# Value and gate columns of a decoder's input projection by seven products per pair of token tiles, with the dilated values kept in DRAM

## What is computed

```python
h = adaLN(RMSNorm(x), c)
proj = h @ w_in            # NSA q | NSA k/v x3 | 24 gates | dilated q | k | v | merge gates
q_n, kv_n, gate_n, qkv_d, merge = jnp.split(proj, IN_SPLITS, axis=-1)
gate_n = sigmoid(gate_n)                       # 3 branches x 8 heads
kc, vc = compress_blocks(...k...), compress_blocks(...v...)   # MLP over blocks of 32 tokens
o_c, o_s = compressed and selected attention(q_n, kc, vc, kv_n[sel])
o_w = banded_attention(q_n, kv_n[win], window 512)
o_nsa = gate_n[0]*o_c + gate_n[1]*o_s + gate_n[2]*o_w
o_dil = dilated_attention(qkv_d)               # 3 groups: strides 1, 4, 16; 4 heads each
x += gate1 * (merge of both mixers); x += gate2 * MoE(adaLN(RMSNorm(x)))
```

## Time and profile before

| | us |
|---|---|
| three executions | 1752.1, 1758.1, 1759.5 (median 1758.1) |
| the profiled execution | 1753.5 |
| its span in the profile | 1751.6 |
| PE busy | 1628.7 (93%) |
| DVE, ACT, POOL busy | 646.8, 406.9, 176.3 |
| projections, queries and keys | about 49 to 290 |
| projections, value part | about 290 to 424 |
| NSA attention | about 426 to 664 |

### The profile page before, as it was taken

The page is one execution under the profiler, slowest core; times in us unless marked ns, Lnnn a source line. Parts: engine busy times, 40 slices in busy tenths (PEclk is TensorE's granted clock), DMA queues, the critical chain, the costliest instruction groups (busy, mean ns, idle before and its releaser), DMA issues. The chain is left out here.

```text
span 1751.6 us, 37114 instructions
## 1 busy us (share of the span) xinstructions
PE 1628.7 (93%) x16025; PEld 1069.8 (61%) x16025; DVE 646.8 (37%) x1594; ACT 406.9 (23%) x908; POOL 176.3 (10%) x220
## 2 busy tenths in 40 slices
PE   5999999999999998999999999999999999998783
PEld 3444445898777786644444445556777767666562
DVE  3533332001767666766655455561000000000003
ACT  4000000001666666610010003221121122111112
POOL 1205000000111110000000000001111111111100
PEclk9999999999999999999999999989999999999996
DMA  9874224131011107334452172169999999999996
GB/s 341 258 230 112 74 84 146 37 104 42 2 44 44 33 2 237 111 111 129 120 145 83 37 280 85 68 258 390 391 383 384 394 387 382 396 392 397 406 385 229
DMA packets 146623, 356.07 MB, mean 203 GB/s; under 512 B 14751, under 2 KB 94231, under 8 KB 121851
## 3 DMA queue, kind: packets, MB, share of 16 engines
q1 hardware_dynamic: 120656, 305.50, 47.0%
q0 software_dynamic: 12656, 28.01, 6.0%
q10 hardware_dynamic: 13148, 20.18, 3.3%
HBM read 320.53 MB, written 45.36 MB: 209 GB/s over the span
## 5 line engine op out<-in xcount | busy, mean ns | idle before, releaser
L2635 PE MATMUL psum<-sb_m_xT,sb_m_ring 128*64 128x64 f32 (+2 forms) x4096 | 152.0, 235 | 22.0 <-issue 17.7
L2635 PEld LDWEIGHTS psum<-sb_m_xT,sb_m_ring 128*64 128x64 f32 x4096 | 147.8, 140 | 35.6 <-issue 34.7
L2384 ACT ACTIVATE sb_m_xT<-psum,sb_rowmod 128x64 f32<-128x64 f32 (+2 forms) x256 | 81.7, 424 | 216.3 <-PE psum L2623 216.3
L2519 DVE TENSOR_TENSOR sb_m_hT<-psum,sb_m_sg 128x256 f32<-128x256 f32 (+2 forms) x32 | 15.3, 477 | 308.9 <-PE psum L2635 308.9
L748 PE MATMUL psum<-sb_vD,sb_room 128*128 128x512 f32 x240 | 104.7, 593 | 0.2 <-DVE sb_vD L685 0.2
L2635 PE MATMUL psum<-sb_m_xT,sb_front 128*64 128x64 f32 (+2 forms) x2560 | 94.5, 236 | 9.9 <-issue 7.3
L2635 PEld LDWEIGHTS psum<-sb_m_xT,sb_front 128*64 128x64 f32 x2560 | 92.4, 142 | 17.2 <-issue 16.9
L1008 ACT ACTIVATE sb_d_probs<-sb_d_probs,sb_d_nmax 128x640 f32<-128x640 f32 (+7 forms) x128 | 92.9, 735 | 1.6 <-DVE sb_d_nmax L1048 1.0
L2642 PE MATMUL psum<-sb_m_ring,sb_m_hT 128*64 128x512 f32 (+2 forms) x256 | 84.5, 611 | 5.6 <-DMA sb_m_ring<-in_exp_w_dram 4.7
L780 PE MATMUL psum<-sb_b_wvd,sb_rows 128*128 128x256 f32 x384 | 88.9, 394 | 0.0
L780 PEld LDWEIGHTS psum<-sb_b_wvd,sb_rows 128*128 128x128 f32 x384 | 84.9, 286 | 3.3
(11 more groups left out here) (384 smaller groups left out, 2408.8 us busy)
## 6 DMA issues: line engine op xcount, KB each, us to landing
sb_m_ring<-in_exp_w_dram SPq DMA_DIRECT2D x48, 2048.0 KB, 34.4
sb_front<-in_exp_w_dram SPq DMA_DIRECT2D x30, 2048.0 KB, 33.8
sb_rows<-in_exp_w_dram SPq DMA_DIRECT2D x18, 2048.0 KB, 36.5
sb_g_ada<-in_ada_w_dram SPq DMA_DIRECT2D x16, 1024.0 KB, 5.3
d_qk<-sb_n_b_sel ACTq DMA_DIRECT2D x20, 512.0 KB, 3.2
sb_front<-in_w_in_dram SPq DMA_DIRECT2D x16, 512.0 KB, 5.4
sb_front<-d_qk SPq DMA_DIRECT2D x15, 512.0 KB, 7.5
sb_n_b_sel<-in_w_in_dram SPq DMA_DIRECT2D x10, 512.0 KB, 8.9
```

The source lines that it names most:

```text
L2384: last = act.activation(dst[:, kk, 0:w], src, ACT.Identity, scale=k.rowmod[:, 0, kk:kk + 1], bias=k.rowmod[:, 1, kk:kk + 1])
L2635: mm = pe.matmul(k.psum[part, which, c * w:(c + 1) * w], view[:, kk, first:first + 2 * CAPS - 1:2], x[:, kk, 0:w], start=(kk == 0), stop=( ...
```

## The change

The value part now also uses seven products in place of eight. It pairs token tile t with tile t + 4 (the two halves of the tokens), the two halves of the channels, and two sets of columns: sets 0 and 1 for the first four pairs (268 columns: 256 values and 12 gates), sets 2 and 3 for the last four (256 columns). The tokens are in natural order everywhere, and the same token sums serve, so `vD` keeps them to the end of the stage. The sums of weights are made by DVE (`v_sums`), for sets 2 and 3 in the midst of the second pair, one of them at the fifth. ACT copies only M1; DVE adds up everything else, into `vS` for set 0 and into four staging buffers for sets 1 to 3, one buffer per product C11, C12, C21, C22. SP stores these to a DRAM array `d_v`, 24 stores of 128 KB, and DVE waits for a buffer's last store before it writes it again. The dilated order is made when the values are read back: 24 loads with 256 bytes per head and token, issued by SP in the NSA stage behind the bias tables of the second pair of heads.

The compression now stands after the fourth pair (its hidden layer) and the fifth (its outputs), and its weights are fetched by SP. The NSA keys, the queries and the first bias tables are issued by SP after the fifth pair's stores. POOL's filling of the ones column of `vD` moves into the NSA stage, where DVE waits for it, and an exponential on a spare column ends ACT's part of the projections.

```diff
-RV = 2 * P + 3 * NSA_H
+RG = 3 * NSA_H // 2
+RV = 2 * P + RG
...
+            sp.wait_ge(s_done, done(npairs - 1, M4))
+            sp.wait_ge(s_used, used(npairs - 1, C21))
+            for kv in range(2):
+                sp.dma_start(w1c[:, kv], k.cmp_w1[0, kv].rearrange("(l p) n -> p l n", p=P)).then_inc(s_cw, 16)
+                sp.dma_start(w2c[:, kv], k.cmp_w2[0, kv].rearrange("(c p) n -> p c n", p=P)).then_inc(s_cw, 16)
             for s in range(2):
                 sp.wait_ge(s_store[s], 16 * npairs)
...
+            for v in range(NV):
+                for c in (C11, C22, C12, C21):
+                    if set_of(v, c) > 0:
+                        t = v % HT + out_tile[c]
+                        sp.wait_ge(s_vused, vused(v, c))
+                        sp.dma_start(k.d_v[set_of(v, c) - 1, t * P:(t + 1) * P, :], staged(c, v)
+                                     ).then_inc(s_vst[SLOT[c]], 16)
+                if v == HT:
+                    sp.wait_ge(s_hid, 4)
...
+                    for c in (C21, C22):
+                        sp.wait_ge(s_vst[SLOT[c]], 16 * stores_of(c, HT - 1))
+                    sp.wait_ge(s_table, 1)
+                    ahead.load_bias(sp, k, 0)
...
+            for v in range(NV):
+                n = width[v // HT]
+                act.wait_ge(s_v, vdone(v, M1))
+                if v >= 1:
+                    act.wait_ge(s_vused, vused(v - 1, U2))
+                act.copy(vm1[:, 0:n], k.psum[:, vbank(v, M1), 0:n]).then_inc(s_vm1, 1)
...
+            act.activation(ahead.last[:, RV:RV + 1], k.vecT[:, 0:1], ACT.Exp).then_inc(s_gates, 1)
...
+            def v_sums(grp):
+                a11, a12, a21, a22 = (x[grp][:, HK * h:HK * (h + 1)] for x in (vx, vy) for h in range(2))
+                dve.wait_ge(s_wv[grp], (64, 32)[grp])
+                sem = s_vsums[grp]
+                dve.tensor_tensor(s1s[grp], a21, a22, ALU.add).then_inc(sem, 1)
+                dve.wait_ge(sem, 1)
+                dve.tensor_tensor(s2s[grp], s1s[grp], a11, ALU.subtract).then_inc(sem, 1)
+                dve.tensor_tensor(a21, a11, a21, ALU.subtract).then_inc(sem, 1)
+                if grp == 0:
+                    dve.wait_ge(sem, 2)
+                    dve.tensor_tensor(s4s[0], a12, s2s[0], ALU.subtract).then_inc(sem, 1)
...
+                def put(c, i, src):
+                    tile = t + out_tile[c]
+                    if grp == 0:
+                        cols = slice(RG, 2 * RG) if c in (C21, C22) else slice(0, RG)
+                        dve.tensor_tensor(graw[:, tile, cols], ps(i)[:, 256:RV], src[:, 256:RV], ALU.add)
+                    if set_of(v, c) == 0:
+                        dve.tensor_tensor(vS[:, tile, :, 0:DH], heads(ps(i)), heads(src), ALU.add).then_inc(s_vused, 1)
+                        return
+                    if stores_of(c, v) >= 2:
+                        dve.wait_ge(s_vst[SLOT[c]], 16 * (stores_of(c, v) - 1))
+                    dve.tensor_tensor(staged(c, v), ps(i)[:, 0:256], src[:, 0:256], ALU.add).then_inc(s_vused, 1)
...
+                if n >= 4:
+                    was, j = divmod(n - 4, 7)
+                    pe.wait_ge(s_vm1 if j == M1 else s_vused, was + 1 if j == M1 else vused(was, last_use[j]))
+                for kk in range(HK):
+                    mm = pe.matmul(k.psum[:, vbank(v, i), 0:width[grp]], x[:, kk, t * P:(t + 1) * P], w[:, kk, :],
+                                   start=(kk == 0), stop=(kk == HK - 1))
...
+            def load_values(sp):
+                for x, stores in enumerate((NT // 2, NT // 2, NT, NT)):
+                    sp.wait_ge(k.s_vst[x], 16 * stores)
+                v0, v1, v2 = (k.d_v[g].rearrange("s (h d) -> s h d", d=DH) for g in range(DIL_G))
+                for t in range(NT):
+                    r, b = divmod(t, 2)
+                    sp.dma_start(vD[:, 0, t, :, 0:DH], v0[t * P:(t + 1) * P]).then_inc(k.s_vd, 16)
+                    sp.dma_start(vD[:, 1, t, :, 0:DH], v1[512 * b + r:512 * b + r + 509:4]).then_inc(k.s_vd, 16)
+                    sp.dma_start(vD[:, 2, t, :, 0:DH], v2[t:t + 8 * (P - 1) + 1:8]).then_inc(k.s_vd, 16)
...
             for i in range(1, PAIRS):
                 if i >= 2:
                     sp.wait_ge(s_biased, before[2 * NT * (i - 1)])
                 ahead.load_bias(sp, k, i)
+                if i == 1:
+                    load_values(sp)
...
             dve.wait_ge(s_clear, 4)
+            dve.wait_ge(s_ones, 1)
```

More of the change, by code:

```diff
@@ L573, in stage_projections, with staged, set_of, stores_of @@
         last_use = {M6: U2, M5: U5, M7: U3, M2: C11, M3: C12, M4: C21}
-        vjobs = [(s, t) for s in range(4) for t in range(NT)]
-        CMP_AT, OUT_AT = 9, 14
+        HT, HK = NT // 2, KD // 2
+        NV = 2 * HT
+        SPLIT = HT - 1
+        flat = spare[:, 0:4, :].rearrange("p a t -> p (a t)")
+        wvy_flat = wvy[:, :, :].rearrange("p k c -> p (k c)")
+        three = lambda at, n: [at[:, HK * n * i:HK * n * (i + 1)].rearrange("p (k c) -> p k c", k=HK) for i in range(3)]
+        vx, vy = [wva, wvd[:, 0]], [wvy, wvd[:, 1]]
+        width = [RV, 256]
+        s1s, s2s, s4s = zip(three(flat, RV), [stage[0].rearrange("p a (k c) -> p (a k) c", k=2),
+                                              stage[1].rearrange("p a (k c) -> p (a k) c", k=2),
+                                              wvy_flat[:, 0:HK * 256].rearrange("p (k c) -> p k c", k=HK)])
+        vm1, vu2, vu5 = (g2row[:, RV * i:RV * (i + 1)] for i in range(3))
+        vu3 = ahead.last[:, 0:RV]
+        SLOT = {C11: 0, C12: 1, C21: 2, C22: 3}
+        def staged(c, v):
+            if v < HT:
+                return ahead.b_sel[0][1][:, 256 * SLOT[c]:256 * (SLOT[c] + 1)]
+            return room[:, 512 * SLOT[c] + 256:512 * SLOT[c] + 512]
+        out_tile = {C11: 0, C12: HT, C21: 0, C22: HT}
+        def set_of(v, c):
+            return 2 * (v // HT) + (c in (C21, C22))
+        vbank = lambda v, i: 4 + (7 * v + i + 2) % 4
+        vdone = lambda v, i: 7 * v + i + 1
+        vused = lambda v, i: 7 * v + i + 1
+        def stores_of(c, v):
+            return sum(1 for w in range(v + 1) if set_of(w, c) > 0)
         block = k.block(mem)
@@ L644, in _ @@
                               ).then_inc(s_store[1], 16)
[L645 to L656, removed]
+            for v in range(NV):
[4 more added lines that the diff above has]
+                act.copy(vm1[:, 0:n], k.psum[:, vbank(v, M1), 0:n]).then_inc(s_vm1, 1)
+                if v == SPLIT:
                     for kv in range(2):
```

190 lines of the change are left out of this document (121 added, 69 removed).

## The result

The changed kernel took 1746.3 us (median of 7 runs, 1741.3 to 1750.3), the kernel before 1755.2 us on the same chip (7 runs, 1752.1 to 1759.5). The ratio is 0.9943, 95% interval 0.9927 to 0.9959: 8.9 us or 0.57% faster. Forecast were 1745.3 us, 1734 to 1753, and "faster" with 0.70. The profiled execution took 1748.9 us, with a span of 1747.1 against 1751.6.

What follows compares the result with a forecast made beforehand. PE was taken to bound the value part, without idle time there. The terms -19.3 + 0.6 + 5.3 + 2.8 + 0.2 gave -10.4 us, from a mean of 1755.7 to 1745.3 us, range 1734 to 1753.

Steps and rivals of the forecast that it cites:

- Products: PE's matmuls in the value part: 224 with tokens in a row take 99.4 us in place of 118.74, -19.3 us.
- About 5: Value part: the share of the products' 19.3 us gain that comes from strided weight loads, in us.
- First pair: Value part, first pair: PE waits for DVE's weight sum s2, some 1.3 us per sum; +0.6 us, bounds 0 and 1.5.
- DVE and ACT per pair: Value part: DVE's sums, under 4 us beside 12 us of PE per pair, and ACT's one copy cost nothing.
- Wait in the seventh pair: PE waits for M2's bank while DVE awaits a store queued behind SP's fourteen loads; +5.3 us, bounds 0 and 8.
- The ground given for it: SP's queue works in order: line 595's four loads landed after 12.7 to 14.9 us, an empty queue's store after 3.1.
- Clock: Behind the seventh pair's wait the granted clock falls to 1.2 GHz, as at NSA's start; +2.8 us, bounds 0 and 3.3.
- End and start: Value stage's end and NSA's start: SP's last store +0.1 and POOL's fifth fill +0.1, together +0.2 us.
- Reading back: NSA stage: 24 loads of 12,288 pieces cost nothing, taking 12 us by bytes or 24 by pieces.
- My bound of 31 ns: Readback in NSA: time per piece on a DMA engine, from SP's queue at 44 to 101 us, pieces of about 505 bytes.
- The doubling to 50 us: Readback in NSA: by the rule for pieces below 512 bytes, an estimate doubles the pieces' time to some 50 us.
- The rival, bias tables too late for the third pair of heads: NSA, SP's queue: the values' loads block these tables; at 6 us each PE waits 31 us, 1776 us; chance 3%.

Runs made afterwards that it cites:

- The kernel with two sets of buffers: The change with a second set of four staging buffers and semaphores for the sixth and eighth pair; 1735.9 us, 0.9884 of the kernel before.
- the stores on ACT: The change with the stores of the sixth to eighth pair issued from ACT's queue, one set of buffers; 1741.3 us, 0.9919 of the kernel before.
- the two comparisons: The change against the kernel before, timed on two chips: 1746.3 against 1755.2 us (0.9943), and 1741.8 against 1754.9 us (0.9923).
- filling the wait: The change with five idle matmuls of 512 columns ahead of M3 of the seventh pair; 1744.0 us, 0.9939 of the kernel before.
- before again: The kernel before, unchanged, run once more on another chip for a second profile; median 1754.9 us, profiled execution 1753.9 us.
- Two kernels with other values in the mixers: Two sets of buffers with the readback replaced by constant 0.5: 1989.7 us; the kernel before with sets 2 and 3 in natural token order: 2000.4 us.

## Why the prediction was right

The forecast's mechanism came about step by step, and each term of the sum has its measured counterpart. One thing it didn't foresee, in NSA, and there the sum was helped by luck (below).

- **Products, -19.3:** measured 4 x 12.65 + 112 x 0.431 = 98.9 us in place of 118.7, -19.8. The kernel with two sets of buffers, where only the first pair's wait is left, shows the same: its value part is 134.2 - 115.0 = 19.2 us shorter than before. The matmuls came 0.452 and 0.428 to 0.431 us apart, where I had 0.454 and 0.433. "About 5" for the strided loads were 5.4, measured by themselves.
- **First pair, +0.6:** 0.43 us, on line 775 as named; the sums took 1.27 us each (forecast: some 1.3).
- **DVE and ACT per pair at nothing:** in PE's rows of the value part no other wait for DVE or ACT is left.
- **Wait in the seventh pair, +5.3:** 5.27 us, and 5.32 the second time. The parts fit too: the loads held SP for 9.8 us (372.19 to 381.99; forecast 9.6), the store landed 23.6 us after the first load's issue (forecast 24.1), and PE went on at 396.4, forecast 394.8 with a start that lay 2.1 us earlier. The ground given for it was weaker than it reads: four loads that land late show full engines as well as an order in the queue. It took the stores on ACT to tell the two apart.
- **Clock, +2.8:** it fell, as the rows of the NSA start suggested, but cost 1.9 us. This was the term that was most off. The low phase was as long as at the start of NSA before, 6.8 us in both places; but there PE was busy nearly throughout (5.7 us by my reading), while here the first 2.6 us fell into the wait and only 4.2 us of M3 and M4 were slowed.
- **End and start, +0.2:** 416.22 - 415.12 = 1.1 us lie between the idle product's end and NSA's first matmul, 0.88 before: +0.2.
- **Reading back, nothing:** leaving it out changed nothing in NSA. The 24 loads of 12,288 pieces were issued within 18 us and landed after 3.3 us in the median:

```profile
DMA packets 13569, 5.10 MB, mean 94 GB/s; under 512 B 13035, under 2 KB 13049, under 8 KB 13561
...
q1 hardware_dynamic: 13561, 4.99, 37.1%
...
sb_vD<-d_v SPq DMA_DIRECT2D x24, 128.0 KB, 3.3
```

These are the DMA rows of 416 to 470 us: 37.1% of 54 us on 16 engines for 13,561 packets is 23.6 ns a packet. My bound of 31 ns held. The Trainium skill, "DMA: Bandwidth & Descriptors", Specifications, says that pieces below 512 bytes don't reach line rate, since the engine then reads, modifies and writes. On the rate the trace agrees: 256 bytes in 23.6 ns are 10.8 GB/s on an engine, 174 on all 16, while the fourteen loads moved 387 GB/s from 392 to 394 us; of the way in which it comes about no run here tells. The doubling to 50 us was my own step on top of it, and the trace doesn't bear it out. The rival, bias tables too late for the third pair of heads, didn't occur: the last of the 24 loads was issued by 437, the tables of the third pair at 473.1, and those of the fourth, which go out when the third pair starts, at 535.4.

Put together, the measured terms make -19.8 + 0.4 + 5.3 + 1.9 + 0.2 = -12.0 us, the forecast was -10.4, and the two comparisons gave -8.9 and -13.1. NSA took 1.2 us longer than in the first execution before, which the forecast had at nothing, and with it the sum is -10.8. So two misses of over a microsecond, on the terms of the value part and on NSA, nearly cancel; that the total came within 1.0 us of the forecast is in part luck, and executions of one kernel differ by more. (The four executions that the forecast starts from have a mean of 1755.8, not 1755.7; it changes nothing.)

Two further points. The first is NSA. Its matmuls are the same in all these kernels, and its length goes with the time that the clock was at half there (the table above). Windows of the change, in which NSA begins at 416.2, and of the kernel before's second execution, in which it begins at 425.3:

```profile
422.00:426.00 4.00, 4.00 (x32) 0.50 1.06 260
426.00:430.00 4.00, 4.00 (x42) 0.76 0.84 189
```

```profile
425.00:429.00 4.00, 1.83 (x17) 1.00 0.66 226
429.00:433.00 4.00, 3.76 (x46) 1.00 0.67 230
```

In that second execution the clock didn't fall at all in NSA, and the stage took 238.1 us; in the first it was at half for 6.8 us and took 240.4. So one and the same kernel differs by 2.3 us in this place. Both executions of the change have the longest low phase, 10.2 us; filling the wait, which takes away the earlier fall and leaves the rest as it is, gave 6.8. This speaks for the reading that the fall in the value part prolongs the one at NSA's start. With one execution of each kernel, and 0, 3.4 or 6.8 us among those without an earlier fall, it is not proven.

The second is the end, 3 us shorter in the first profile of the kernel before than in all others. It has not been explained; it has nothing to do with the change, as before again shows (573.2).

## What to carry to other kernels

Where a matmul kernel is bound by PE without gaps, count records and their spacing, and look at the weight loads' own length: strided tokens made matmuls of 256 columns 10% slower (0.472 against 0.431 us). A small store that someone waits for should not stand behind large loads in one queue. A second set of buffers was the surest remedy here; another engine's queue worked, with 1.2 us to spare, and brought its own waits with it. The rearrangement through DRAM (3 MB) cost nothing that could be seen, issued behind what is needed next and with a whole stage before its use. And where stages are compared between executions, read the granted clock beside them: here differences of up to 3.5 us in NSA go with it.

## What the runs showed of the hardware

- With a wait of 5.3 us TensorE's granted clock went from 1.00 to 0.50 (2.4 to 1.2 GHz), which cost 1.9 us beyond the wait. With five idle products within it the clock stayed at 1.00, and with a wait of 2.2 us by itself too.
- At the start of NSA, with the same matmuls each time, the clock was at 0.50 for 0 to 10.2 us, and the stage took 238.1 to 241.6 us accordingly; two executions of one kernel had 0 and 6.8.
- A store of 128 KB took 1.7 us where nothing else moved, 7.9 to 10.4 us from ACT's queue beside SP's fourteen loads, and 13.8 us in SP's queue behind the same loads. From ACT's queue a store issued 3 us after a load landed 6 us before it.
- Float32 weight loads took 190 ns with tokens in a row and up to 339 ns with every fourth or eighth token (median of all 332); 128 matmuls of 256 columns took 5.4 us longer with them.
- Loads in pieces of 256 bytes took 23.6 ns a piece on an engine, less than the 31 ns of the pieces of about 505 bytes; byte for byte that is slower, 10.8 against 16 GB/s on an engine.
- Two kernels with other values in the mixers took some 250 us more (1989.7 against 1735.9, 2000.4 against 1754.9), nearly all of it behind the router, so that such an experiment tells only of the stages ahead of it here.
